# Products that nobody reads, put in front of TensorE's waits in a two-block transformer kernel

## The reference

```python
def first_block(x, c, ...):
    x = layer_ab(...)   # norm, modulate, input projection, RG-LRU and sparse attention, output projection,
                        # norm, modulate, swiglu
    x = layer_c(...)    # norm, modulate, projections, attention over chosen keys, output projection, norm, swiglu
    return rmsnorm(x, final_norm)

def second_block(x, ...):
    for l in range(2):
        # norm and modulate both streams; low-rank keys, values and queries, each with norms of their own;
        # Fourier mixing, gated MLP, attention, output projection; then for both streams (layer 1: only x)
        x = x + g2 * expert_choice_moe(modulate_2(x, sh2, sc2), ...)

def rms_norm(x):
    return x * lax.rsqrt(jnp.mean(x * x, axis=-1, keepdims=True) + EPS)

def expert_choice_moe(h, w_router, w_gate, w_up, w_down):
    aff = jax.nn.softmax(jnp.einsum('bnd,de->bne', h, w_router), axis=-1)
    g, idx = lax.top_k(jnp.swapaxes(aff, 1, 2), cap)      # 16 experts, each chooses 32 tokens
    ...
```

## Time and profile before

| what | value |
|---|---|
| median of 3 runs | 1832.7 us (1826.36 to 1834.37) |
| the profiled execution: its time, its span | 1833.32 us, 1831.5 us |
| busy share of the span | PE 88%, DVE 39%, ACT 18%, POOL 4% |
| mean granted TensorE clock | 0.935 of full speed |
| HBM read over the span | 441.20 MB |

### The profile page before, as it was taken

The page is one execution under the profiler, slowest core; times in us unless marked ns, Lnnn a source line. Parts: engine busy times, 40 slices in busy tenths (PEclk is TensorE's granted clock), DMA queues, the critical chain, the costliest instruction groups (busy, mean ns, idle before and its releaser), DMA issues.

```text
span 1831.5 us, 22406 instructions
## 1 busy us (share of the span) xinstructions
PE 1613.7 (88%) x9499; PEld 1173.8 (64%) x9499; DVE 714.6 (39%) x1633; ACT 324.4 (18%) x774; POOL 79.8 (4%) x92
## 2 busy tenths in 40 slices
PE   6998999999998999999798988699998698886555
PEld 4784778888775788888667857545354475742122
DVE  2224267777226287775342242302023325211002
ACT  3032310000215100000232232310000314210000
POOL 0002200000005000000001020000000002000000
PEclk9987999999989999999899998699999799989888
DMA  9637469886842656885333325099997523579997
GB/s 362 212 126 254 175 250 345 321 326 227 261 135 93 230 197 217 297 306 171 117 135 128 135 95 229 1 378 409 408 409 288 180 92 138 229 300 409 409 409 286
DMA packets 168536, 443.69 MB, mean 242 GB/s; under 512 B 7755, under 2 KB 21237, under 8 KB 168437
## 3 DMA queue, kind: packets, MB, share of 16 engines
q1 hardware_dynamic: 168068, 442.13, 64.9%
q10 hardware_dynamic: 368, 0.13, 0.0%
HBM read 441.20 MB, written 1.05 MB: 241 GB/s over the span
## 4 chain that ended last, share of the span: by engine, by line
PE 68%; DMA 8%; DVE 7%; issue 3%; POOL 2%; ACT 2%; PEld 1%; PEldq 0%; ACTq 0%; SPq 0%; DVEq 0%
PE bank L666 66%; DMA scr<-in_w_up 4%; DMA ring<-in_w_gate 3%; POOL scr L1855 2%; PE bank L677 2%; DMA ring<-in_w_down 1%; DVE scr L1903 1%; PEld bank L666 1%; DVE xT L2432 1%; DVE scr L1911 1%; DVE scr L2303 0%; DVE ctxT L2432 0%; DVE scr L2390 0%; ACT scr L1525 0%; DVE small L2389 0%
## 5 line engine op out<-in xcount | busy, mean ns | idle before, releaser
L666 PE MATMUL bank<-hT,ring 128*128 128x256 f32 (+1 forms) x2576 | 515.8, 391 | 22.6 <-ACT hT L1533 21.0
L666 PEld LDWEIGHTS bank<-hT,ring 128*128 128x128 f32 (+1 forms) x2576 | 420.6, 182 | 115.0 <-issue 37.5
L666 PE MATMUL bank<-scr,ring 128*128 128x256 f32 (+3 forms) x1604 | 353.8, 382 | 14.4 <-DVEq L2271 5.8
L666 PEld LDWEIGHTS bank<-scr,ring 128*128 128x128 f32 (+2 forms) x1604 | 293.0, 192 | 64.8 <-issue 17.6
L1969 DVE SCALAR_TENSOR_TENSOR scr<-scr,csil 128x512 f32<-128x512 f32 x420 | 290.9, 748 | 3.2
L666 PE MATMUL bank<-scr 128*32 128x512 f32 (+8 forms) x1504 | 208.8, 434 | 15.2 <-issue 3.6
L666 PEld LDWEIGHTS bank<-scr 128*32 128x32 f32 (+4 forms) x1504 | 131.9, 160 | 87.4 <-issue 64.6
L666 PE MATMUL bank<-ring,scr 128*32 128x512 f32 (+2 forms) x1344 | 161.2, 589 | 16.1 <-DMA ring<-in_w_down 11.9
L1855 POOL TENSOR_SCALAR scr<-scr,small 128x256 f32<-128x256 f32 (+2 forms) x88 | 79.6, 922 | 1476.0 <-DVE small L2019 1303.0
L666 PEld LDWEIGHTS bank<-ring,scr 128*32 128x32 f32 (+2 forms) x1344 | 59.2, 115 | 110.2 <-issue 87.2
L2440 DVE TENSOR_TENSOR brow<-brow,bank 128x512 f32<-128x512 f32 x12 | 7.9, 686 | 245.6 <-ACT brow L1823 245.6
(11 more groups left out here) (244 smaller groups left out, 1095.4 us busy)
## 6 DMA issues: line engine op xcount, KB each, us to landing
ring<-in_w_gate SPq DMA_DIRECT2D x25, 2048.0 KB, 18.7
ring<-in_w_down SPq DMA_DIRECT2D x25, 2048.0 KB, 23.8
scr<-in_w_ada SPq DMA_DIRECT2D x23, 2048.0 KB, 8.7
scr<-in_w_up SPq DMA_DIRECT2D x21, 2048.0 KB, 23.6
scr<-in_l_mod_w SPq DMA_DIRECT2D x14, 2048.0 KB, 16.1
ring<-in_w_up SPq DMA_DIRECT2D x11, 2048.0 KB, 15.8
ring<-in_l_mod_w SPq DMA_DIRECT2D x10, 2048.0 KB, 9.8
ring<-in_l_ffn_wg SPq DMA_DIRECT2D x10, 2048.0 KB, 13.5
```

What stands on the lines that cost most here:

```text
L666: ins = nc.tensor.matmul(out, lhsT, rhs, start=start, stop=stop, skip_group_check=True)
```

## The change

A new helper `stay_busy(count)` on TensorE issues `count` products of `ones` (128x128) by the first 256 columns of the table `tab`, all into one bank of DVE's, and signals nothing. Nobody reads them. It takes the bank that is next in turn without counting it, and waits until DVE has read what stood there. It is called:

- with 15 at the end of each `norm` (the first norm of the kernel, four norms of `mixers`, three of `route`);
- with 15 at the end of `finish` behind the two output projections of the first block, and with `15 * layer`, so none and 15, behind its two feed-forward parts;
- with 8 in the two attentions of the first block, behind the scores of unit 2;
- with 8 at the start of `spread_keys_rms`, ahead of its wait;
- with 18 in `route`, behind `turn_tokens(1)` and ahead of the wait for DVE's choice.

That is 267 products: 120, 45, 16, 32 and 54.

```diff
+            def stay_busy(count):
+                if n["dve"] >= 2:
+                    pe.wait_ge(dve_read, n["dve"] - 1)
+                b = banks[n["dve"] % 2]
+                for _ in range(count):
+                    nc.tensor.matmul(b[:, 0:T], ones[:, :], tab[:, 0:T], start=True, stop=True, skip_group_check=True)
...
             def norm(sq, modulated=True):
                 b = bank_for_act()
                 for i in range(DC):
                     sum_squares(b, sq, i)
+                stay_busy(15)
...
-            def finish(parts, sq, modulated=True):
+            def finish(parts, sq, modulated=True, busy_after=0):
...
                 n["x"] += DC
+                if busy_after:
+                    stay_busy(busy_after)
...
-                finish([(w[:, k, :], y[:, 4 + k, :]) for k in range(4)], sq)
+                finish([(w[:, k, :], y[:, 4 + k, :]) for k in range(4)], sq, True, 15 if sq is not None else 0)
...
-                        finish([(wdp[:, k, :], actT[:, f % 4, :])], hT, modulated)
+                        finish([(wdp[:, k, :], actT[:, f % 4, :])], hT, modulated, 15 * layer)
...
                         S(i, banks[4 + u % 2 * 2:6 + u % 2 * 2])
+                    if i == 2 and busy_before:
+                        stay_busy(busy_before)
...
-            attention(len(units), S, V, lambda i: 2 * (units[i][0] + 1), pt, pr)
+            attention(len(units), S, V, lambda i: 2 * (units[i][0] + 1), pt, pr, 8)
...
-            attention(len(units1), S1, V1, lambda i: 2 * (units1[i][0] + 1), pt1, pr1)
+            attention(len(units1), S1, V1, lambda i: 2 * (units1[i][0] + 1), pt1, pr1, 8)
...
                 def spread_keys_rms():
+                    stay_busy(8)
                     from_dve()
...
                 turn_tokens(1)
+                stay_busy(18)
                 from_dve()
```

More of the change, by code:

```diff
@@ L929, in ffn, with attention @@
                 settle()
-            def attention(N, S, V, n_blocks, pt_, pr_):
+            def attention(N, S, V, n_blocks, pt_, pr_, busy_before=0):
                 u0 = n["unit"]
```

## The result

The changed kernel takes 1845.0 us (median of 5 runs, 1842.4 to 1856.1), the kernel before 1831.3 (median of 5). The ratio is 1.0101, 95% interval 1.0079 to 1.0123, so +14 us by the medians and +18 us by the ratio. Forecast were 1852 us and +19.8, range 1837 to 1867: slower, and by about this much. The two profiled executions differ by less, 9.1 us of span (1831.5 and 1840.6): that of the kernel before was one of its slower runs, that of the change its fastest.

A forecast was written before the change was run, and what follows sets the result against it. TensorE's own products were taken as the bound, two thirds of the span. Terms 2.6 + 1.9 - 0.1 + 1.4 + 2.7 + 2.6 + 8.7 = 19.8 us on 1833.3, standing 0.6 above the median, gave 1852 us, range 1837 to 1867.

The forecast's parts named there:

- A dummy costs 0.43 us, and 15 of them 6.5.: At 2.4 GHz, two instructions of 0.216 us per dummy product; 15 put 6.5 us into a norm's 3.50 us pause.
- The rival with 0.216 per product: Everywhere: dummies cost half, 15 fit the 3.50 us pause, about -33 us, so 1800; chance 0.08 with other faster ways.
- +3.0 at a norm: Behind norms with products right behind them: 15 dummies delay those products by 3.0 us, and full clock pays some back.
- First norm: Kernel's first norm: first chunk comes at 41.7, +4.0 less possible clock gain, +2.6 us, between +1.3 and +4.
- Keys' norm: At `spread_keys_rms`: 8 dummies give +1.8 us at three, +0.6 at the fourth, less clock gains; +2.7 us together.
- Attentions: First block's two attentions: 8 dummies each, partly covered by POOL's work; +2.6 us for both, +8 without cover.
- a POOL stretch of unchanged length: In the attentions: sign that would confirm the forecast, POOL working as long as before despite the 8 dummies.
- The routings, +8.7: Three routings: 18 dummies end after DVE's choice; +3.3 us and twice +2.7, or -0.6 at full clock throughout.
- the 18 dummies start low for about 4.6 us: In the routings: dummies begin at 1.2 GHz, adding 2.3 us, so the turn of DVE's answer comes +4.5 us.
- third sign of being wrong: In the routings: stretches at 0.50 gone altogether, and DVE's answer turned less than 3 us later from the sums.
- norms behind the output projections: Two norms in the first block: +3.0 us each, less 1.6 and 2.5 of clock; +1.9 us together.
- last feed-forward part and the norm behind it: Dummies +0.1, sums at full clock -1.5, the norm's own dummies +3.0, low stretch gone -1.7; -0.1 us.

The follow-up runs named there:

- e1: The change with every dummy product 128 columns wide in place of 256, counts kept; 1813.9 us, ratio 0.9911 to the kernel before.
- e4: The change with only its bursts of 15, without its 8s and 18s; 1835.5 us, ratio 1.0032 to the kernel before.
- e9: The change with only its bursts of 15, each made an 8, no other dummies; 1813.9 us, ratio 0.9893 to the kernel before.
- e6: The change with only the 8 dummies in each of the first block's two attentions; 1832.7 us, ratio 1.0006 to the kernel before.
- e5: The change with only the 18 dummies ahead of the choice in all three routings; 1836.2 us, ratio 1.0042 to the kernel before.
- e2: The change with every dummy product 8 columns wide in place of 256, counts kept; 1844.1 us, ratio 1.0070 to the kernel before.
- e3: The change with full-width dummies cut to counts that fit the pauses, none at the first norm or attentions; 1805.2 us, ratio 0.9869 to the kernel before.
- second profile: Profile from measuring the unaltered change once more; that measurement gave 1846.1 us, ratio 1.0080 to the kernel before.
- e8: The change with counts fitted to the pauses, plus bursts in pauses that were still empty; 1801.1 us, ratio 0.9838 to the kernel before.
- e7: The change with only the 8 dummies at the keys' norm, four times; 1838.8 us, ratio 1.0036 to the kernel before.

## Why the prediction was right

**A dummy costs 0.43 us, and 15 of them 6.5.** Measured 6.48. This decided the sign. The rival with 0.216 per product is out; what it would have brought is seen in e1, where the product was really made to cost half: -16 us, not the -33 that the rival named, because the routings kept low stretches (3.9 us won there, not 18).

**+3.0 at a norm, paid back by 1.6 to 3.0 of clock.** From the last sums to the next products the pause is 3.0 longer, and the products behind are shorter by 1.8 to 3.1: 14.32 us for 80 instructions where 14.4 was worked out. e4 measured the sum of these terms, with +6 us, and e9 that the length beyond the pause is what costs. One row is misnamed in the prediction: the 16.09 belongs to the norm behind the last feed-forward part. The x norm of layer 1 has this one in the kernel before, which gives the same -3.0:

```profile
1470.60 17.41 PE L666 MATMUL bank<-hT,ring 128*128 128x256 f32 x80 [3.50 <-ACT hT L1533]
```

**First norm.** The first product on the chunks starts at 41.62 in place of 37.70, where 41.7 was worked out:

```profile
41.62 20.70 PE L666 MATMUL bank<-hT,ring 128*128 128x256 f32 x87 [1.38 <-ACT hT L1549]
```

In both profiles of the change the clock gives back 1.0 us in the products up to 60 us.

**Keys' norm.** +1.8 was worked out for one burst, +1.9 measured.

**Attentions.** Right in size as far as e6 can tell, wrong in a detail. I had POOL working through, and "a POOL stretch of unchanged length" was a sign to look for. It is not there: in the changed kernel POOL stands still for 2.22 us in the first attention and 0.51 in the second:

```profile
175.07 7.22 POOL L1871 TENSOR_SCALAR scr<-scr,small 128x256 f32<-128x256 f32 x8 [174.65 <-DVE small L2033]
184.51 10.70 POOL L1871 TENSOR_SCALAR scr<-scr,small 128x256 f32<-128x256 f32 x14 [2.22 <-DVE small L2033]
...
572.51 7.22 POOL L1871 TENSOR_SCALAR scr<-scr,small 128x256 f32<-128x256 f32 x8 [370.65 <-DVE small L2035]
580.24 16.52 POOL L1871 TENSOR_SCALAR scr<-scr,small 128x256 f32<-128x256 f32 x24 [0.51 <-DVE small L2035]
```

So the scores of unit 3 come a little too late for it. In the second attention the end is late by the same 0.5 us. For the first it is not shown: between its start and the output projection the change's two profiles lose 3.4 and 0.9 us, and e5, with no dummy there, loses 1.2.

**The routings, +8.7, were the most mis-sized term.** In the two profiles of the change they cost about +1.6 and +4.7: to the 1.5 and 4.6 of layer 0 above comes 0.1 of layer 1. The step that failed is that the 18 dummies start low for about 4.6 us. They took 7.93 to 8.81 us, 8.28 in the first routing, where 10.1 was assumed and 7.8 is full clock. TensorE turns DVE's answer 1.7 to 3.3 us later from the sums than before, not 4.5. The reason behind the step was right in five of six routings. In the first routing of the first profile the windows over the router, the turns, and the dummies read

```profile
1143.86:1147.35 3.49, 3.49 (x33) 3.49 (x32) 0.00 (x0) 1.14 (x1) 0.00 (x0) 1.00 0.73 292
1147.35:1151.06 3.71, 3.17 (x21) 2.85 (x20) 2.25 (x10) 1.78 (x4) 0.00 (x0) 0.63 0.00 1
1151.06:1159.27 8.21, 8.21 (x38) 6.94 (x37) 4.17 (x13) 1.87 (x2) 0.00 (x0) 0.96 0.01 3
```

and over the turns of the second routing

```profile
1177.20:1179.83 2.63, 2.09 (x19) 1.83 (x19) 1.49 (x7) 1.43 (x4) 0.00 (x0) 1.00 0.00 0
```

In the first the clock fell in the turns, behind the narrow products, and came back some 0.7 us behind the dummies' start: a mean of 0.63 over 3.71 us is 2.7 us at 0.50, a mean of 0.96 over 8.21 is 0.7, so it was low for 3.4 us in all. I had taken the length from stretches that were low for long. In the second routing it did not fall at all from the router through the dummies, and the answer is turned 1.7 us later: there the prediction's own third sign of being wrong came true. The gathering of the second routing won 2.3 us (4.04 for 6.36) in the first profile and 0.8 (5.57) in the second, where 1.8 was assumed. What the Trainium skill says of transposes (TensorE: Matmul & The Clock Gate, Part 4: PE-mode transpose), that they do not count as busy for the clock, fits the 0.63 in the turns, but the narrow products ahead of them explain it as well, and the 1.00 in the second routing's turns shows that such a stretch does not always bring the clock down; no run here separates the two. e2 shows that narrow products alone do not hold it.

**The sum.** Matched product by product, the two profiles of the change compare with the kernel before, stretch by stretch, as follows (us, plus is later):

| stretch | forecast | first profile | second profile |
|---|---|---|---|
| start to the first attention (first norm) | +2.6 | +2.6 | +4.0 |
| both attentions | +2.6 | +3.9 | +1.5 |
| norms behind the output projections | +1.9 | +1.4 | +1.4 |
| from the first of these norms to the second attention | none | -1.4 | -1.4 |
| last feed-forward part and the norm behind it | -0.1 | -0.5 | -0.5 |
| the other norms of `mixers`, keys' norms | +4.1 | +1.3 | +1.5 |
| routings | +8.7 | +1.6 | +4.7 |
| the rest | none | +0.2 | +0.2 |
| sum | +19.8 | +9.1 | +11.3 |

So the sign and the mechanism are shown (e4 against e9), and the size came out near the ratio's +18 partly by luck. The routings were put 4 to 7 us too high and the norms and keys of layer 1 some 2.6 too high (the sums behind its first keys' norm won 3.0 us, not 1.8), and one gain of 1.4 was not foreseen. Nor do the profiles reach the +14 of the medians: the profiled run of the kernel before is 2.0 us above its median, that of the change 2.6 below. What makes the slower runs slower is open beyond their lower mean clock.

## What to carry to other kernels

A product that nobody reads is free only inside a pause, so count it in the trace before choosing how many: here one float32 product was two instructions and 0.43 us, and making the bursts nearly twice as long as their pause, with nothing else changed, turned a gain of 18 to 20 us (e9) into a loss of 6 (e4). Fill a pause with wide products to just its length. I would put none where there is hardly a pause (the attentions) or where other work already stands there (the first norm); for the attentions alone no difference could be measured. If the clock is already low when a burst starts, it takes longer and overruns sooner: 18 dummies took 7.9 us at full clock and 8.7 in e5, and the eight-column ones of e2 took 7.69 at 1.2 GHz, in a pause of 4.3.

## What the runs showed of the hardware that was not expected

- At the norm behind the second output projection, 30 instructions of 128 columns in a pause of 3.5 us kept the granted clock (1.00 behind them); 30 of 8 columns, with TensorE as busy (3.51 and 3.41 us), did not (a mean of 0.81 behind them): 14.05 us for 64 instructions behind the former, 8.83 for 32 behind the latter. At six norms of six it was the same way.
- A shorter time of the products behind a burst is not always the clock. The router's 32 narrow instructions took 3.64 us behind the 15 dummies, and in e3 4.88 behind 8, at a granted clock of 1.00 in both:

```profile
1114.85 3.62 PE L722 MATMUL bank<-tab,ones 128*128 128x256 f32 x16
1117.87 3.30 ACT L1549 ACTIVATE scr<-scr,mods 128x256 f32<-128x256 f32 x8 [2.34 <-DVE scr L1927]
1118.52 4.88 PE L666 MATMUL bank<-csil,scr 128*128 128x16 f32 x32
```

Behind 8 the first half of the router runs at the pace at which ACT makes the chunks (2.95 us for 16 instructions, 1.79 for the other 16); behind 15 the chunks are all there (1.70 and 1.79). So a burst that is too long gets part of its delay back without any clock.
- Whether the clock holds from there through the whole router varied with the same burst. Behind 8 full-width dummies the router took 4.88, 5.06 and 4.88 us in e3, 4.88, 6.56 and 6.73 in e8, and 5.93, 4.89 and 4.88 in e9; behind the half-width ones of e1 6.75, 6.73 and 5.35.
- The same program's runs spread more than I had taken: 1842 to 1856 us for the change, 1827 to 1854 for e2 and 1827 to 1849 for e7. The mean granted clock of single runs of the change went from 0.969 at 1842.4 us to 0.950 at 1856.1, in order, so the spread goes with the clock. Part of it lies where nothing was changed: 7.0 us in the modulation's products in e9's profile.
